# A third z buffer, unforced output transposes and norm squares on ScalarE in a planned attention and convolution kernel

## The chip, the cores and the metric

The kernel runs on the 8 cores of one Trainium2 chip. Each core takes half of the query rows of one of the four batch elements: 2048 own rows out of 4096. The cores don't exchange data. The metric is device time in microseconds (us) of the slowest core, as the median of several runs. A core has TensorE (PE, with its weight loads listed apart as PEld), VectorE (DVE), ScalarE (ACT), GpSimd (POOL) and SyncE (SP); TensorE, VectorE and ScalarE share eight banks of PSUM, each 512 float32 wide.

## What is computed

```python
h = rms_norm(x, g_pre)
q, k, v, z_a, cb, cc, cx, z_c, ga, gc = split(h @ w_in)
# branch A: 4 heads, two softmax maps each, ALiBi, causal
a = softmax(q0 @ k0.T) - lam * softmax(q1 @ k1.T)
o = rms_norm(a @ v, subln_gain) * (1 - lam_init)
y_attn = (o * silu(z_a)) @ w_attn_o
# branch B: width-3 causal depthwise convolution
u = conv3(cc * cx)
y_conv = (cb * u * silu(z_c)) @ w_conv_o
# merge
y = sigmoid(ga + b_a) * y_attn + sigmoid(gc + b_c) * y_conv
out = x + rms_norm(y @ w_out, g_post)
```

x has 4 x 4096 rows of 1024; q, k, v and z_a are 512 wide, the convolution has 512 channels.

## The kernel before

The program has four stages: normalisation and the k, q, v projections (to about 157 us in the profiled run), attention with everything of the convolution branch as filler (to about 547 us), the merge (to about 713 us), and the output projection.

The attention stage is written by a planner that runs while the program is built. It keeps an estimated clock for each engine (`p.now`), gives each instruction an estimated duration (`t=`), and so fixes the order of each engine's queue. What was estimated plays no part on the chip: there each queue runs in order and waits on semaphores.

**Groups and units.** `GROUPS` (L1038) are 16 pairs of four query blocks s and head h, in the order (3,2) (0,2) (3,3) (0,3) (3,0) (0,0) (3,1) (0,1) (2,2) and so on, numbered 0 to 15 here. A group is a run of units, each a few key blocks. The loop at L1344 emits for unit n: the scores of unit n+1 (`put_qk`, L1099), the value products of unit n (`emit_av`, L1159), filler until unit n+1's exponentials should be done (`put_fill`), then the exponentials of unit n+1 on ScalarE (L1128), with a mask on VectorE (L1140) where the unit is on the diagonal. Scores use banks 0 to 3, sums of value products banks 4 to 6. A group of s = 0 has three units, all of them masked; every other group ends in a unit without a mask.

**Filler.** `Filler` (L243) is a list of tiles; one is open at a time, and in this stage all share bank 7. A tile is some matmuls and a `post` that evicts the bank: convolution projections (L823, 8 matmuls of 512 columns, evicted at L980, L984, L1006 or, over a tanh at L1014, L1016), small halo tiles (L954), z gates (L858, 32 matmuls of 128 columns, evicted by a tanh on ScalarE, L870, and a multiply on VectorE, L872, then L878), norm tiles (L907, 16 matmuls of 2 columns), and output transposes (L1239, 4 of them, evicted at L1246). Evictions that need ScalarE are put into `hot` and emitted by `run_hot`, when the next tile opens or after the next exponentials. Taps and gates of the convolution wait in `chain`, the steps of a finished group's normalisation in `side`; `put_pieces` (L1317) places both into VectorE's free time.

**End of a group.** At a group's last unit the loop calls `drain(g - 2)`, which emits all that is left in `side` of the group two back: four sums of squares (L1213), the root (L1219, L1221, and L1223 on GpSimd), four gates (L1231), and the push of the transposes. `epilogue` (L1176) then first steps the filler until the transposes of group g - 2 are out, and emits the VectorE instructions that read banks 4 to 6 (L1186 to L1204) and so free them for the next group. z and the gates have two buffers each, by g % 2. The z tile of a group is pushed at its first unit if nothing of group g - 2 is left in `side`, else as soon as that is so.

**Norm squares and the fork.** Before group 4 (`FORK`, L1277) the program forks: if a bound on the products of the norms of k and q (heads 0 and 1) holds, a version that skips far key blocks runs. For the bound, 24 pieces of 512 columns are squared on GpSimd (L898, called from L1369 at each unit before the fork, as far as GpSimd's estimated clock allows); each four make a norm tile (L907) that is reduced on VectorE (L914); after six of these, a two-matmul tile (L931), three VectorE instructions (L938 to L943), and one register load per engine (`load_way`, L1169). At the unit before the fork a loop (L1361) makes what is still missing:

```python
if n + 1 == FORK:
    while not way:
        squares_of(1.0e9)
        fill.step()
        run_hot()
    load_way()
    p.mark()
```

The squares have two buffers, `sq[i % 2]`, and a new norm tile is inserted behind the first entry of the filler's list.

Of the kernel before, what the change touches and what calls it, by code (L numbers as in the profile page):

```python
# [289 lines left out]
def build_program():  # L290
# [23 lines left out]
    with contextlib.ExitStack() as st:  # L314
# [4 lines left out]
        def emission(p, skip):  # L319
# [90 lines left out]
            sz = [reg(sz_off + i * 2 * K, 2 * K, F32).rearrange("p (b n) -> p b n", b=4) for i in range(2)]  # L410
# [12 lines left out]
            tz_off = take(2 * K)  # L423
            tz = reg(tz_off, 2 * K, F32)
# [53 lines left out]
            for i in range(2):  # L478
                for d in range(4):
                    p.place(("hTp", i, d), htp_off[i], 8 * K)  # L480
                p.apart([("hTp", i, d) for d in range(4)])
                p.place(("prod", i), pr_off[i], 2080)
                p.place(("ut", i), u_off[i], 2 * K)
                p.place(("tt", i), t_off[i], 2 * K)
                p.place(("zr", i), zr_off[i], 2 * K)
                p.place(("sz", i), sz_off + i * 2 * K, 2 * K)
# [4 lines left out]
            p.place(("tz",), tz_off, 2 * K)  # L491
            for i in range(NR):
                p.place(("ring", i), ring_off[i], 2 * K)
# [356 lines left out]
            def z_tile(s, h, g):  # L850
                tb = g % 2
# [39 lines left out]
            def squares_of(until):  # L891

                while pieces and not kq_left and pieces[0][0] < 2 + len(normed) and p.now["pool"] < until:
                    i, t = pieces.pop(0)
                    what, h, kd = NORMS[i]
                    src = KT[h][:, kd * 2048 + t * 512:kd * 2048 + (t + 1) * 512] if what == "k" else QT[h][:, t * 512:(t + 1) * 512]
                    name = ("KT", h, kd, t) if what == "k" else ("QT", h, t)
                    p.op("pool", (lambda e, i=i, t=t, src=src: e.tensor_tensor(out=sq[i % 2][:, t * 512:(t + 1) * 512], in0=src, in1=src, op=ALU.mult)),  # L898
                         reads=[name], writes=[("sq", i % 2, t)], t=1.35)
                    if t == 3:  # L900
                        fill.q.insert(min(1, len(fill.q)), norm_tile(i))

            def norm_tile(i):
# [9 lines left out]
                def post(bk):  # L913
                    p.op("dve", (lambda e: e.tensor_reduce(out=S_NM[:, i:i + 1], in_=bank(bk)[:, 0:32], axis=mybir.AxisListType.X, op=ALU.max)),  # L914
                         reads=[("bank", bk)], writes=[("nm", i)], t=0.2)
                    normed.append(i)
                    if i == len(NORMS) - 1:
                        for a, lo, hi in ((0, 0, 4), (1, 4, 6)):
                            p.op("dve", (lambda e, a=a, lo=lo, hi=hi: e.tensor_reduce(out=S_KQ[:, a:a + 1], in_=S_NM[:, lo:hi],
                                                                                     axis=mybir.AxisListType.X, op=ALU.max)),  # L920
                                 reads=[("nm", x) for x in range(lo, hi)], writes=[("kqm", a)], t=0.15)
                        p.op("dve", (lambda e: e.tensor_scalar(out=nmb, in0=S_KQ, scalar1=1.01, scalar2=None, op0=ALU.mult)),
                             reads=[("kqm", 0), ("kqm", 1)], writes=[("nmb",)], t=0.15)
                        fill.q.insert(min(1, len(fill.q)), way_tile())
                return {"mm": mm, "post": post, "n": 16, "w": 0.057}

            def way_tile():
# [17 lines left out]
                return {"mm": mm, "post": post, "n": 2, "w": 0.057}  # L945
# [230 lines left out]
            def epilogue(s, h, g):  # L1176
                ob = g % 2
                while g >= 2 and g - 2 not in t_done:
                    fill.step()
# [46 lines left out]
                def gate(qb):  # L1226
                    while g not in z_done:
# [4 lines left out]
                                                                  in1=sz[ob][:, qb, :], op0=ALU.mult, op1=ALU.mult)),  # L1232
                         reads=[("oraw", ob, qb), ("rs", ob), ("sz", ob)], writes=[("gat", ob, qb)], t=0.345)

                def trans():
# [12 lines left out]
                    tile_ = {"mm": mm, "post": post, "n": 4, "w": 0.057}  # L1248
# [7 lines left out]
                for qb in range(4):  # L1256
                    side.append((g, 0.35, lambda qb=qb: gate(qb), [("rs", ob), ("sz", ob), ("z", g)]))
# [6 lines left out]
            def open_z(names):  # L1264

                return all(n[1] in z_done and not hot and not any(n in c_[0] for c_ in chain) for n in names if n[0] == "z")
# [28 lines left out]

            def put_fill(until):
# [6 lines left out]
                while now["pe"] < until or credit - took[0] > 0.0:  # L1303
                    if not fill.open:

                        free = p.unread(("bank", 7))
                        if hot or (free > now["pe"] + 0.15 and free + 0.2 > until):
                            break
                    if fill.left() <= TAIL:
                        break  # L1310
                    one()
# [29 lines left out]
            z_wait = None  # L1341
            put_qk(0)
            put_exp(0)
            for n in range(NU):  # L1344
                s, h, segs, first, last = units[n]
                if first:
                    started = set()
                    if g:
                        z_wait = (s, h, g)
# [3 lines left out]
                if z_wait and not any(x[0] <= g - 2 for x in side):  # L1353
                    fill.push(z_tile(*z_wait))
                    z_wait = None
# [12 lines left out]
                elif n < FORK:  # L1368
                    squares_of(now["pe"] + 0.6)  # L1369
# [245 lines left out]
```

How the kernel before makes its waits and increments, by code:

```python
    def replay(self, eng_name, engine, part, waited):  # L181
        cut = self.parting[eng_name]
        for o in self.ops[eng_name][:cut] if part == 0 else self.ops[eng_name][cut:]:
            need = {}
            for d in o.waits:
                s, v = d.token
                if v > need.get(s, 0):
                    need[s] = v
            for s in sorted(need):
                v = need[s]
                if waited.get(s, 0) >= v:
                    continue
                engine.wait_ge(self.sems[s], v)
                waited[s] = v
            ins = o.fn(engine)
            if o.token is not None:
                ins.then_inc(self.sems[o.token[0]], 16 if o.dma is not None else 1)
# [9 lines left out]
    def play(name, e):  # L207
        waited = {}
        r = e.alloc_register("way_" + name)
        fast.regs[name] = r
        fast.replay(name, e, 0, waited)
        with e.If_cmp(r, 1, "IS_GE"):
            fast.replay(name, e, 1, dict(waited))
        with e.If_lt(r, 1):
            general.replay(name, e, 1, dict(waited))
        if name == "sp":
            assert [o.token for o in fast.final_ops] == [o.token for o in general.final_ops]
            for o in fast.final_ops:
                e.wait_ge(fast.sems[o.token[0]], o.token[1])
```

## Time and profile before

| what | us |
|---|---|
| median of 3 runs (777.16 to 779.83) | 779.58 |
| the profiled execution | 780.28 |
| its span, core 4, the slowest | 778.7 |
| spans of the other cores | 772.3 to 778.1 |
| TensorE busy, core 4 | 724.1 |
| attention stage, about 157 to 547 us | 390 |

The profiled execution has 1.6 us outside the span of its slowest core. In the answers of the trace a line such as L1239 is a line of the kernel; "idle before <-" gives the time that the engine stood still before the instruction and the instruction whose end released it. PEclk is the granted clock of TensorE as a share of its full 2.4 GHz; its other level is 1.2 GHz, so 0.92 over a stretch means that part of it ran at the lower level.

### The profile page before, as it was taken

How to read it: one execution, taken by the hardware profiler on the slowest of the kernel's cores; microseconds unless marked ns; L12 is line 12 of the kernel's file. 1: busy time of each engine (PE TensorE's matmuls, PEld its weight loads, DVE VectorE, ACT ScalarE, POOL GpSimd, SP SyncE). 2: the span in 40 equal slices, each digit the busy share in tenths (PEclk: the TensorE clock that was granted, in tenths of full speed). 3: DMA queues.
4: the chain of work that ended last, by engine and by line, in shares of the span. 5: the costliest groups of instructions: out<-in, count | busy, mean ns of one | idle time of the engine just before them, and what ended most of it. 6: DMA issues, size and time to landing. Idle time of an engine off the chain costs nothing.

```text
span 778.7 us, 15293 instructions; the slowest of 8 cores (772.3 to 778.7 us)
## 1 busy us (share of the span) xinstructions
PE 724.1 (93%) x5370; PEld 382.2 (49%) x5370; DVE 368.8 (47%) x829; ACT 377.5 (48%) x552; POOL 152.5 (20%) x165
## 2 busy tenths in 40 slices
PE   4799999998888998799999999899999999999995
PEld 1354444455555454455555556555444444444442
DVE  3666444222654456657565467746522222222444
ACT  2446555264565654376666667675222222223433
POOL 1100000105711000010100001101333332321663
PEclk9999999998999999899999999999999999999998
DMA  7997973810000110000100101002852222200786
GB/s 166 246 209 203 252 168 68 128 22 2 2 2 29 28 18 12 2 15 15 29 2 2 28 2 28 3 1 56 134 123 41 41 42 40 42 1 1 247 293 221
DMA packets 39684, 57.68 MB, mean 74 GB/s; under 512 B 23825, under 2 KB 24209, under 8 KB 39346
## 3 DMA queue, kind: packets, MB, share of 16 engines
q1 hardware_dynamic: 31682, 39.58, 18.4%
q0 software_dynamic: 7776, 16.78, 13.8%
q8 instruction: 47, 0.77, 0.4%
q14 instruction: 35, 0.29, 0.1%
q10 hardware_dynamic: 144, 0.26, 0.1%
HBM read 59.76 MB, written 8.39 MB: 88 GB/s over the span
## 4 chain that ended last, share of the span: by engine, by line
PE 84%; DVE 7%; issue 4%; ACT 2%; DMA 1%; DVEq 0%; POOL 0%; SPq 0%; ACTq 0%; POOLq 0%
PE psum L1428 14%; PE psum L823 13%; PE psum L1159 12%; PE psum L725 11%; PE psum L711 8%; PE psum L1481 7%; PE psum L1435 7%; PE psum L1099 6%; PE psum L858 4%; ACT arena L1128 2%; DVE arena L1199 1%; PE psum L688 1%; DVE arena L1204 1%; PE psum L1239 1%; DMA arena<-gpre 1%
## 5 line engine op out<-in xcount | busy, mean ns | idle before, releaser
L1128 ACT ACTIVATE arena<-psum 128x1024 bf16<-128x1024 f32 (+2 forms) x259 | 219.0, 902 | 112.5 <-PE psum L1099 111.9
L1159 PE MATMUL psum<-arena 128*128 128x130 bf16 x1780 | 134.0, 223 | 5.3 <-DVE arena L1199 2.8
L1159 PEld LDWEIGHTS psum<-arena 128*128 128x128 bf16 x1780 | 106.0, 99 | 54.2 <-issue 47.9
L823 PE MATMUL psum<-arena 128*128 128x512 bf16 x512 | 126.3, 389 | 5.7 <-DVE arena L1186 2.1
L1428 PE MATMUL psum<-arena 128*128 128x512 bf16 x512 | 115.7, 379 | 0.0
L1440 ACT ACTIVATE arena<-psum,arena 128x512 f32<-128x512 f32 x64 | 44.0, 687 | 120.4 <-PE psum L1428 120.4
L1444 DVE SCALAR_TENSOR_TENSOR arena<-arena,psum 128x512 f32<-128x512 f32 x64 | 43.8, 687 | 115.8 <-PE psum L1435 115.8
L725 PE MATMUL psum<-arena 128*128 128x512 bf16 x384 | 88.4, 379 | 0.0
L1099 PE MATMUL psum<-arena 64*128 64x512 bf16 (+3 forms) x568 | 73.8, 340 | 6.3 <-ACT arena L1128 3.9
L1428 PEld LDWEIGHTS psum<-arena 128*128 128x128 bf16 x512 | 50.1, 98 | 60.2
L823 PEld LDWEIGHTS psum<-arena 128*128 128x128 bf16 x512 | 47.6, 99 | 54.9 <-issue 12.6
L711 PE MATMUL psum<-arena 128*128 128x512 bf16 x256 | 64.0, 394 | 5.2 <-DVE arena L643 4.2
L1447 POOL TENSOR_TENSOR arena<-arena 128x512 bf16<-128x512 f32 x32 | 40.4, 1262 | 116.6 <-DVE arena L1444 116.6
L1435 PE MATMUL psum<-arena 128*128 128x512 bf16 x256 | 60.5, 379 | 0.0
L725 PEld LDWEIGHTS psum<-arena 128*128 128x128 bf16 x384 | 37.0, 98 | 42.9 <-issue 0.4
L1481 PE MATMUL psum<-arena 128*128 128x512 bf16 x256 | 57.0, 387 | 0.0
L740 ACT CAST arena<-psum 128x512 bf16<-128x512 f32 x42 | 24.5, 584 | 58.5 <-PE psum L725 58.5
L1223 POOL TENSOR_TENSOR arena<-arena 128x4 f32<-128x4 f32 x16 | 18.8, 1176 | 148.1 <-DVE arena L1221 142.8
L716 DVE TENSOR_TENSOR arena<-psum,arena 128x512 bf16<-128x512 f32 x32 | 22.1, 691 | 51.6 <-PE psum L711 51.4
L645 DVE SCALAR_TENSOR_TENSOR arena<-arena 128x1024 bf16<-128x1024 f32 (+1 forms) x33 | 42.4, 1284 | 3.4
L711 PEld LDWEIGHTS psum<-arena 128*128 128x128 bf16 x256 | 25.0, 100 | 37.0 <-issue 9.8
L630 ACT ACTIVATE arena<-arena 128x1024 bf16<-128x1024 f32 (+1 forms) x33 | 34.9, 1058 | 15.1 <-DMA arena<-x_perm 15.1
(101 smaller groups left out, 626.3 us busy)
## 6 DMA issues: line engine op xcount, KB each, us to landing
arena<-x_perm SPq DMA_DIRECT2D x48, 512.0 KB, 6.4
arena<-w_chunk POOLq DMA_DIRECT2D x40, 256.0 KB, 4.8
out_own<-arena SPq DMA_DIRECT2D x15, 512.0 KB, 4.7
arena<-w_y POOLq DMA_DIRECT2D x8, 256.0 KB, 5.5
arena<-wo_r POOLq DMA_DIRECT2D x1, 2048.0 KB, 20.6
arena<-w_wide POOLq DMA_DIRECT2D x4, 256.0 KB, 11.4
arena<-w_wide POOLq DMA_DIRECT2D x1, 1024.0 KB, 11.9
arena<-gpost SPq DMA_DIRECT2D x1, 512.0 KB, 3.6
```

Of the source, the lines that this page charges most:

```text
L645: p.op("dve", (lambda e: e.scalar_tensor_tensor(out=xn[nb][0:rows, :], in0=xring[b][0:rows, :], scalar=rs0[0:rows, n:n + 1], in1=gpre[0:ro ...
L711: p.op("pe", (lambda e, kc=kc: e.matmul(bank(bk), lhsT=h_blk(n, kc), rhs=wv[kc // 2][:, kc % 2, :], start=(kc == 0), stop=(kc == KC - 1))) ...
L725: p.op("pe", (lambda e: e.matmul(bank(bk), lhsT=w[:, kc, :], rhs=rhs, start=(kc == 0), stop=(kc == KC - 1))), reads=[("w" + what, h)] + h_ ...
L823: p.op("pe", (lambda e: e.matmul(bank(bk), lhsT=lhs(kc), rhs=rhs(kc), start=(kc == 0), stop=(kc == n - 1))), reads=rd, writes=[("bank", bk)])
L1099: p.op("pe", (lambda e, kd=kd, m=m, kcol=kcol, q0=q0, c0=c0, w=w: e.matmul(psum[:, 2 * kd + m, c0 * 128:(c0 + w) * 128], lhsT=KT[h][64 * m ...
L1128: p.op("act", (lambda e, a0=a0, a1=a1, c0=c0, c1=c1, bias=bias: e.activation(out=PT[sl][:, a0:a1, c0 * 128:c1 * 128], in_=psum[:, a0:a1, c ...
L1159: p.op("pe", (lambda e, kd=kd, m=m, cb=cb, acc=acc, first=first, vj=vj: e.matmul(acc, lhsT=PT[sl][:, 2 * kd + m, cb * 128:(cb + 1) * 128], ...
L1428: p.op("pe", (lambda e, sl=sl, bk=bk, kc=kc: e.matmul(bank(bk), lhsT=ring[sl][:, kc, :], rhs=hTo[:, kc, t * 512:(t + 1) * 512], start=(kc ...
L1435: p.op("pe", (lambda e, br=br, bk=bk, c=c, src=src: e.matmul(bank(bk), lhsT=ring[sy][:, 4 * br + c, :], rhs=src[:, c, t * 512:(t + 1) * 51 ...
L1440: p.op("act", (lambda e, br=br: e.activation(out=tmp[ts[br]], in_=bank(bs[br]), func=AF.Tanh, scale=0.5, bias=bm[:, 8 * br + j:8 * br + j ...
L1444: p.op("dve", (lambda e, br=br: e.scalar_tensor_tensor(out=tmp[ts[br]], in0=tmp[ts[br]], scalar=1.0, in1=bank(bs[2 + br]), op0=ALU.add, op ...
L1481: p.op("pe", (lambda e, j=j, half=half: e.matmul(bank(b0 + half), lhsT=yT[:, j, i * 128:(i + 1) * 128], rhs=wo[:, j, half * 512:(half + 1) ...
```

## The change

It has five parts. A third z buffer of 2 KB is placed at the end of the side region; z tiles and gates take it by g % 3, and the z tile of a group is pushed at the group's first unit, always. `epilogue` no longer steps the filler until the transposes of g - 2 are out; instead a gate of group g does that before it is emitted, and `open_z` keeps gates out of VectorE's free time until then. Norm, way and transpose tiles name what they need; when a slot opens and the first tile of the list has inputs that the planner expects more than 0.1 us later, the first tile that names no needs goes ahead (`next_ready`). The squares are made on ScalarE, and the call at each unit before the fork is gone, so that the loop at the fork makes all of them; the end of the norms is told by their number. `put_fill` no longer opens a tile while bank 7 is read for more than 0.15 us to come; before it did where the bank would be free 0.2 us before the time up to which it fills.

```diff
@@ z buffers
+            NZ = 3
+            sz_at = [sz_off, sz_off + 2 * K, take(2 * K)]
+            sz = [reg(a, 2 * K, F32).rearrange("p (b n) -> p b n", b=4) for a in sz_at]
...
             def z_tile(s, h, g):
-                tb = g % 2
+                tb = g % NZ
...
             def squares_of(until):
-                while pieces and not kq_left and pieces[0][0] < 2 + len(normed) and p.now["pool"] < until:
+                while pieces and not kq_left and (pieces[0][0] < 2 or pieces[0][0] - 2 in normed) and p.now["act"] < until:
...
-                    p.op("pool", (lambda e, i=i, t=t, src=src: e.tensor_tensor(out=sq[i % 2][:, t * 512:(t + 1) * 512], in0=src, in1=src, op=ALU.mult)),
-                         reads=[name], writes=[("sq", i % 2, t)], t=1.35)
+                    p.op("act", (lambda e, i=i, t=t, src=src: e.activation(out=sq[i % 2][:, t * 512:(t + 1) * 512], in_=src, func=AF.Square)),
+                         reads=[name], writes=[("sq", i % 2, t)], t=0.58)
...
-                    if i == len(NORMS) - 1:
+                    if len(normed) == len(NORMS):
...
-                return {"mm": mm, "post": post, "n": 16, "w": 0.057}
+                return {"mm": mm, "post": post, "n": 16, "w": 0.057, "need": [("sq", i % 2, t) for t in range(4)]}
...
             def epilogue(s, h, g):
                 ob = g % 2
-                while g >= 2 and g - 2 not in t_done:
-                    fill.step()
...
                 def gate(qb):
-                    while g not in z_done:
+                    while g not in z_done or (g >= 2 and g - 2 not in t_done):
                         fill.step()
...
-                    tile_ = {"mm": mm, "post": post, "n": 4, "w": 0.057}
+                    tile_ = {"mm": mm, "post": post, "n": 4, "w": 0.057, "need": [("gat", ob, qb) for qb in range(4)]}
...
             def open_z(names):
-                return all(n[1] in z_done and not hot and not any(n in c_[0] for c_ in chain) for n in names if n[0] == "z")
+                return all(n[1] in z_done and (n[1] < 2 or n[1] - 2 in t_done) and not hot and not any(n in c_[0] for c_ in chain)
+                           for n in names if n[0] == "z")
...
+            def next_ready():
+
+                if p.when(fill.q[0].get("need", [])) > now["pe"] + 0.1:
+                    later = [k for k, t in enumerate(fill.q) if "need" not in t]
+                    if later:
+                        fill.q.insert(0, fill.q.pop(later[0]))
...
-                    if not fill.open:
-
-                        free = p.unread(("bank", 7))
-                        if hot or (free > now["pe"] + 0.15 and free + 0.2 > until):
-                            break
+                    if not fill.open and (hot or p.unread(("bank", 7)) > now["pe"] + 0.15):
+                        break
                     if fill.left() <= TAIL:
                         break
+                    if not fill.open:
+                        next_ready()
...
                     if g:
-                        z_wait = (s, h, g)
+                        fill.push(z_tile(s, h, g))
...
-                if z_wait and not any(x[0] <= g - 2 for x in side):
-                    fill.push(z_tile(*z_wait))
-                    z_wait = None
...
                 elif n < FORK:
-                    squares_of(now["pe"] + 0.6)
                     if way:
                         load_way()
```

## Rows read from the trace of the kernel before

**Rows 1.** The page: busy time by engine; shares of the chain that ended last.

```profile
PE 724.1 (93%) x5370; PEld 382.2 (49%) x5370; DVE 368.8 (47%) x829; ACT 377.5 (48%) x552; POOL 152.5 (20%) x165
...
PE 84%; DVE 7%; issue 4%; ACT 2%; DMA 1%; DVEq 0%; POOL 0%; SPq 0%; ACTq 0%; POOLq 0%
```

**Rows 2.** Busy time by stretch, core 4: stretch, length, engines, PEclk, DMA share, GB/s.

```profile
176.00:278.00 102.00, 90.98 (x966) 58.09 (x966) 48.45 (x117) 58.08 (x67) 31.14 (x32) 0.92 0.05 12
278.00:330.00 52.00, 43.00 (x371) 23.41 (x368) 33.31 (x90) 23.76 (x37) 4.00 (x7) 0.90 0.07 11
330.00:540.00 210.00, 198.08 (x2116) 120.93 (x2115) 124.74 (x357) 142.36 (x175) 19.75 (x28) 1.00 0.08 13
36.00:176.00 140.00, 140.00 (x762) 65.85 (x761) 63.90 (x103) 71.18 (x133) 5.65 (x12) 1.00 0.72 151
```

**Rows 3.** PE's waits, 174 to 278: line, releaser, us in total, times, longest.

```profile
PE psum L907 <- DVE arena L962: 2.3, 1, 2.3
PE psum L1099 <- DVE arena L943: 1.8, 1, 1.8
```

**Rows 4.** In order of time, GpSimd's squares, then three VectorE instructions: start, us.

```profile
175.66 8.65 POOL L898 TENSOR_TENSOR arena<-arena 128x512 bf16<-128x512 bf16 x8 [23.92 <-PE psum L725]
...
180.62 1.35 DVE L1140 TENSOR_TENSOR arena<-arena 128x512 bf16<-128x512 bf16 x1 [0.22 <-ACT arena L1128]
181.89 1.52 DVE L878 TENSOR_TENSOR arena<-arena 128x512 f32<-128x512 f32 x1
...
226.83 0.68 DVE L878 TENSOR_TENSOR arena<-arena 128x512 f32<-128x512 f32 x1
```

**Rows 5.** In order of time, PE at the first norm tile: start, us, [idle before].

```profile
184.06 0.62 PE L907 MATMUL psum<-arena 128*128 128x2 bf16 x16 [2.29 <-DVE arena L962]
...
187.74 3.36 PE L823 MATMUL psum<-arena 128*128 128x512 bf16 x8
```

**Rows 6.** In order of time, ScalarE and PE around the fork.

```profile
276.93 1.08 ACT L1128 ACTIVATE arena<-psum 128x512 bf16<-128x512 f32 x2
277.83 0.71 PE L1099 MATMUL psum<-arena 64*128 64x384 bf16 x8
278.63 1.28 ACT L1128 ACT_TABLE_LOAD   x1 [0.62 <-PE psum L1099]
...
281.55 1.89 PE L823 MATMUL psum<-arena 128*128 128x512 bf16 x8 [0.72 <-DVE arena L1186]
```

**Rows 7.** In order of time, ScalarE: four 512-column exponentials; the first output block.

```profile
290.66 2.06 ACT L1128 ACTIVATE arena<-psum 128x512 bf16<-128x512 f32 x4 [0.40 <-PE psum L1099]
...
716.72 1.02 ACT L1490 ACTIVATE arena<-psum 128x1024 bf16<-128x1024 f32 x1 [4.49 <-PE psum L1481]
...
717.97 1.28 ACT L1506 ACT_TABLE_LOAD   x1
```

**Rows 8.** PE at the bound's last step; SyncE's register load and its next instruction.

```profile
232.18 0.27 PE L931 MATMUL psum<-arena 128*1 128x128 bf16 x2
...
235.16 1.04 PE L1099 MATMUL psum<-arena 64*128 64x512 bf16 x4 [1.84 <-DVE arena L943]
...
L1169 SPq TENSOR_LOAD <-arena x1: 467/467/467, 234.4 to 234.4; - x1
...
235.03 0.33 SPq L530 DMA_DIRECT2D arena<-gpost  x1
```

**Rows 9.** In order of time, the ends of groups 4 and 5: PE, then VectorE.

```profile
301.87 0.38 PE L1239 MATMUL psum<-arena 128*128 128x128 bf16 x4 [2.47 <-DVE arena L872]
...
319.48 3.57 PE L823 MATMUL psum<-arena 128*128 128x512 bf16 x8 [0.68 <-DVE arena L1186]
...
299.71 1.14 DVE L1231 SCALAR_TENSOR_TENSOR arena<-arena 128x128 bf16<-128x128 f32 x4 [1.35 <-POOL arena L1223]
...
319.25 0.16 DVE L1186 TENSOR_REDUCE arena<-psum 128x6 f32<-128x12 f32 x1
```

**Rows 10.** PE's waits, 278 to 547: line, releaser, us in total, times, longest.

```profile
PE psum L1239 <- DVE arena L872: 7.0, 4, 3.6
```

More of the change, by code:

```diff
@@ L409, in emission @@
             sz_off = take(4 * K)
-            sz = [reg(sz_off + i * 2 * K, 2 * K, F32).rearrange("p (b n) -> p b n", b=4) for i in range(2)]
             gc_off = take(16 * K)
@@ L485, in emission @@
                 p.place(("zr", i), zr_off[i], 2 * K)
-                p.place(("sz", i), sz_off + i * 2 * K, 2 * K)
             p.place(("wz",), wz_off, 8 * K)
@@ L491, in emission @@
             p.place(("tz",), tz_off, 2 * K)
+            for i in range(NZ):
+                p.place(("sz", i), sz_at[i], 2 * K)
             for i in range(NR):
@@ L944, in post @@
                                     reads=[("prodn",)], writes=[("way",)], t=0.15))
-                return {"mm": mm, "post": post, "n": 2, "w": 0.057}
+                return {"mm": mm, "post": post, "n": 2, "w": 0.057, "need": [("nmb",)]}
             def halo_tile(c):
@@ L1231, in gate @@
                     p.op("dve", (lambda e: e.scalar_tensor_tensor(out=gat[ob][:, qb, :], in0=oraw[ob][:, qb, :], scalar=RS[:, qb:qb + 1],
-                                                                  in1=sz[ob][:, qb, :], op0=ALU.mult, op1=ALU.mult)),
-                         reads=[("oraw", ob, qb), ("rs", ob), ("sz", ob)], writes=[("gat", ob, qb)], t=0.345)
+                                                                  in1=sz[g % NZ][:, qb, :], op0=ALU.mult, op1=ALU.mult)),
+                         reads=[("oraw", ob, qb), ("rs", ob), ("sz", g % NZ)], writes=[("gat", ob, qb)], t=0.345)
                 def trans():
@@ L1256, in epilogue @@
                 for qb in range(4):
-                    side.append((g, 0.35, lambda qb=qb: gate(qb), [("rs", ob), ("sz", ob), ("z", g)]))
+                    side.append((g, 0.35, lambda qb=qb: gate(qb), [("rs", ob), ("sz", g % NZ), ("z", g)]))
                 side.append((g, 0.0, trans, []))
@@ L1352, in emission @@
                     drain(g - 2)
-                if z_wait and not any(x[0] <= g - 2 for x in side):
-                    fill.push(z_tile(*z_wait))
-                    z_wait = None
                 credit += max(0.0, fill.left() + late - TAIL - credit) * work[n] / rest_work
```

## The prediction

> **What bounds the kernel now.** First the page: TensorE is busy for 724.1 of 778.7 us and carries 84% of the chain that ended last [rows 1]. So only TensorE's idle time and its time at the lower clock can be won or lost. Then the table by stretch, for where these lie: from 36 to 176 us TensorE never stops (140.00 of 140.00), and the change touches nothing there; the loss is in attention [rows 2]. I split that stage in three, each loss being idle time plus what the granted clock took, worked out as length times (1 - PEclk):
> - 176 to 278, up to the fork: 11.0 idle and 8.2 of clock, 19.2 us.
> - 278 to 330, groups 4 and 5: 9.0 idle and 5.2 of clock, 14.2 us.
> - 330 to 540: 11.9 idle, no clock, which is 5.7% and serves as the norm for undisturbed attention.
>
> Last TensorE's waits, for what ended the idle time. Before the fork they are those around norm tiles and the register load [rows 3], afterwards above all the transposes that wait for VectorE [rows 10].
>
> **The squares before the fork: removed.** Eight squares hold GpSimd for 8.65 us, and there are three such runs [rows 4]. Meanwhile VectorE's two-input instructions take about twice as long: L878 takes 1.52 us beside them and 0.68 without [rows 4]. One such delay holds the bank under the first norm tile, which stands 2.29 us [rows 5]; behind it eight matmuls of 512 columns take 3.36 us [rows 5] against 1.89 [rows 6], which is the 1.2 GHz level. All this goes, and so does the 1.84 us wait for the register load in this place [rows 8]. What can be won at most is the stretch's loss less the norm: 19.2 - 0.057 x 79 (102 less the loss and some 4 us of norm tiles) = 14.7 us. From below: the two waits of rows 3 with what the clock took from the tile behind the first (3.36 - 1.89 = 1.5) make 4.1 + 1.5 = 5.6, say 6. The ends of groups 0 to 2 remain in either kernel, so I take 10.5.
>
> **The squares at the fork: added.** The call at each unit is gone, so all 24 pieces are emitted by the loop ahead of the fork, that is behind the exponential at 276.93 and ahead of the scores at 277.83 [rows 6]. Neither the next scores nor the value products of the last unit of group 3 are emitted until the loop ends: this is a serial chain between ScalarE, TensorE and VectorE, with nothing of attention beside it.
> - Squares: four 512-column exponentials take 2.06 us [rows 7], 0.52 each, so eight take 4.2 us. The row reads PSUM and the squares read SBUF; the first output block's Square takes 1.02 for 1024 columns [rows 7], so twice the number is excluded. Two buffers allow eight pieces at once, hence three rounds, 12.6 us.
> - The list then holds one convolution tile, norm tile 1, norm tile 0, the next convolution tile, and so on: four convolution tiles, T0 to T3, six norm tiles (0.62 each [rows 5]) and the way tile.
> - Between rounds: last square, the rest of a norm tile, its reduction, the first matmuls of the other norm tile, ScalarE again. A reduction of 0.2 us and four semaphore crossings of about 0.1 come to 1.2 us. Meanwhile the convolution tile and its eviction must also be done: at the lower clock 3.36 + 0.95 for the copy and its semaphores, with a norm reduction ahead, which is 0.4 longer than the squares. So 1.6, twice.
> - End: two norm tiles with reductions, 1.9; T3 at 3.36 with 0.95; the way tile's 0.27, and from its end at 232.45 to TensorE's next start behind the load 2.71 in the row [rows 8], of which some 0.85 is queueing and other work on VectorE. I take 1.9.
>
> Sum: 12.6 + 3.2 + 1.9 + 4.3 + 0.3 + 1.9 = 24.2, and 25 with one tanh eviction that has to queue behind squares on ScalarE. TensorE does useful work in it: 4 x 1.73 of convolution (a row of 1.89 less the drain) and 3.6 of norm and way tiles, which the old kernel does too: 10.5. The loss is 14.5 us, and about 2.5 for the restart at the lower clock, since the tile behind the wait in rows 9 loses 3.57 - 1.89 = 1.7 by itself. I take 17. Bounds: 11, if the clock stays up (T3 1.5 less, the gaps 0.8 less), no tanh stands in it (0.8 less) and the restart costs nothing: 25 - 3.1 - 10.5; 22, if every round ends in a tanh behind squares and the restart takes 4.
> The branch right after the load costs little: SyncE's load begins at 234.4 and takes 0.467, and its next instruction, which stands behind the fork, starts at 235.03 [rows 8].
>
> Does Square need another function table? The first output block's Square at 716.72 follows the merge's tanh without a table load, and the load of 1.28 comes only ahead of the square root [rows 7]. So none is added. The Trainium skill, ScalarE: Activation LUTs, section Table sets: the hidden batching unit, asks to group calls by table set, because each switch costs about 2.7 us, and its table does not name the set of Square. By that rule, with Square in a set of its own, two switches would add some 5.3 us to the chain and give 789 us; the row speaks against it.
>
> **Unforced transposes, z first, the third buffer.** The buffer itself costs 2 KB and no instruction. z first is the same work earlier. The transposes waited 7.0 us for z's eviction, 2.47 and 3.6 of it at the ends of groups 4 and 5 [rows 9, 10]; behind each a fill tile waits 0.68 and then runs at the lower clock [rows 9]. Gross, that is most of the 14.2 us of this stretch. What is late next is VectorE: at the last unit `drain(g - 2)` still emits sums of squares, root and gates ahead of the epilogue, and the gates wait 1.35 for GpSimd's root [rows 9]. The next group's value products wait for that epilogue, at 319.25 in group 5 [rows 9]; without the z multiply and the transposes' copy ahead of it, it comes about 1.9 earlier, no more. TensorE then stands there instead of ahead of the transposes. I take +1 for group 4, +2 for group 5 and +3 for the smaller waits later. Floor 0; ceiling 12, which is 14.2 less the norm for 38 us.
>
> The new wait, a gate of g for the transposes of g - 2, finds them done: they have a whole group more, and behind a gate on VectorE's queue stand only the epilogue and the mask of the next unit.
>
> **No opening on a busy bank.** Where the planner waited for bank 7 under an epilogue, it filled that time: at 281.55 it stood 0.72 and then worked 1.89 [rows 6]. Now it breaks, and TensorE stands until scores or sums are free, some 1.8. I charge 1.1 each for groups 1, 3 and 7 and 0.2 for smaller places: 3.5. Bounds 0 and 5. With the 6 above, the two parts together give +2.5, bounds -5 and +12. `next_ready` costs nothing: norm tiles are only stepped by the fork's loop, which does not call it, and a transpose that is passed over loses nothing.
>
> **The sum.** Against the profiled 780.28: -10.5 (squares gone) + 17 (chain at the fork) - 2.5 (ends of groups) = +4.0, 784.3. The median of the runs is 0.7 lower, so on its terms 783.6 us.
>
> **Rivals.**
> - *The ends of groups pay in full, and it is faster.* z no longer sits in bank 7 when the transposes want it, VectorE finds time for a finished group's steps before the last unit, and the clock doesn't fall. For it: VectorE is busy for only 33.31 of 52 us there [rows 2]. Against it: the root's trip to GpSimd stands in VectorE's queue. It pays 12 instead of 2.5: -10.5 + 17 - 12 = -5.5, 774 us. It decides from a gain above 10.4 at these ends, where the sum passes -3.9.
> - *The chain is covered, and nothing much changes.* The clock stays up and the fork costs its lower bound: -10.5 + 11 - 2.5 = -2, 778 us. For it: three of the four tiles run while ScalarE squares. Against it: TensorE works for 10.5 us of 22 at best, and PEclk fell before the fork already where it stood for 2.29 us [rows 5].
> - *The stall moves to the epilogue everywhere.* Groups end on VectorE, fill is refused there, and before the fork only the lower bound comes back: 17 - 6 + 3 = +14, 794 us.
>
> **How the numbers follow.** Forecast 0.50, with a range of its own of 778 to 789; ends pay in full 0.24; covered chain 0.13; stall at the epilogue 0.13. A measurement of this kernel tells about 0.5%, 3.9 us, from no change, so faster means below 775.7 and slower above 783.5. Of the forecast 0.27 lies above, 0.22 within and 0.01 below; the rival at 774 gives 0.19 to faster and 0.05 to no change, that at 778 0.03 and 0.10, that at 794 all to slower. Faster 0.23, same 0.37, slower 0.40. The range reaches to the rivals on both sides, 773 to 793, and leaves out the far halves of both.
>
> **What would show it.** Between two exponentials at about 275 (the fork comes some 10 us earlier) ScalarE has 24 squares in three runs of eight, with 20 us or more from the first to the register load, and TensorE is idle for 12 or more of the 25. Before it, L878 and L1140 keep their short times, PEclk is near 1.00, and no norm tiles lie between units. At the ends of groups 4 and 5 the waits of transposes are gone and value products wait for L1199 and L1204. I would be wrong if convolution tiles filled the fork, if the clock stayed up through it, or if the ends of groups had no wait at all.

## The result and the profile after

The changed kernel takes 813.4 us (median of 4 runs, 811.25 to 814.58) against 779.4 before: 1.0439 times as long, 95% interval 1.0408 to 1.0470, 34 us slower. Here and below a time is the median of a kernel's fast executions; in a few others the cores of one die ran at a lower granted clock and took over 30 us longer, and some expectations quote a median that takes one of these in and lies up to 1 us higher. The forecast was 783.6 and its range ended at 793. The sign was right, the size wrong by a factor of eight.

The page of after has the lines that answer to [rows 1]:

```profile
PE 729.0 (90%) x5370; PEld 388.8 (48%) x5370; DVE 363.7 (45%) x829; ACT 388.7 (48%) x576; POOL 126.2 (16%) x141
...
PE 79%; ACT 6%; issue 5%; DVE 5%; DMA 3%; POOL 0%; DVEq 0%; SPq 0%; ACTq 0%; POOLq 0%
```

TensorE works as long as before (729.0 against 724.1), but 82 us of the span are idle, where 55 were, and ScalarE now has 6% of the chain. Lines are 3 higher than before in this kernel, by some lines less: L826 is the old L823, L1102 the old L1099, L1131 the old L1128, L1162 the old L1159, L1200 the old L1199, L1240 the old L1239.

The table by stretch of after, as in [rows 2]: stretch, length, engines, PEclk, DMA share, GB/s. The cuts are the start of the loop at the fork, its end, the end of groups 4 and 5, and the last value product.

```profile
157.00:263.00 106.00, 98.85 (x1011) 58.68 (x1010) 46.41 (x113) 68.46 (x77) 4.95 (x8) 1.00 0.04 7
263.00:293.00 30.00, 19.80 (x168) 9.13 (x166) 6.76 (x22) 15.05 (x29) 1.24 (x3) 0.61 0.14 22
293.00:350.00 57.00, 42.76 (x405) 29.37 (x403) 29.20 (x86) 27.47 (x42) 3.49 (x5) 0.81 0.02 8
350.00:563.00 213.00, 186.46 (x1989) 117.55 (x1988) 116.70 (x340) 136.15 (x169) 17.35 (x25) 0.98 0.07 11
563.00:581.00 18.00, 18.00 (x87) 8.20 (x85) 13.90 (x37) 1.70 (x3) 3.21 (x7) 1.00 0.30 56
```

The fourth line is the surprise: 213 us of plain attention with 26.5 us idle, where the old kernel lost 11.9 of 210 [rows 2]. TensorE's waits say to what. Before first, then after (line, releaser, us in total, times, longest):

```profile
PE psum L1099 <- ACT arena L1128: 3.9, 12, 1.0
PE psum L1159 <- DVE arena L1199: 2.8, 5, 1.1
```

```profile
PE psum L1102 <- ACT arena L1131: 27.8, 45, 1.8
PE psum L1162 <- DVE arena L1200: 14.1, 7, 4.1
```

Scores now wait 45 times for the exponentials that free their banks, and value products seven times for the epilogue. Transposes no longer appear, where they waited 7.0 us for z [rows 10]. One of the 45, in order of time on PE (start, us, [idle before]):

```profile
310.09 1.89 PE L826 MATMUL psum<-arena 128*128 128x512 bf16 x8
311.81 0.39 PE L1162 MATMUL psum<-arena 128*128 128x130 bf16 x4
312.14 0.61 PE L1102 MATMUL psum<-arena 64*128 64x512 bf16 x4
312.67 0.63 PE L1162 MATMUL psum<-arena 128*128 128x130 bf16 x8
315.05 0.61 PE L1102 MATMUL psum<-arena 64*128 64x384 bf16 x8 [1.75 <-ACT arena L1131]
```

VectorE evicts the convolution tile of 310.09 from 312.91 to 313.60, so its bank is still read when the next slot comes at 313.3. No tile is opened, so TensorE has nothing to do until 315.05. What was not done is left for the end of attention. Again before, then after:

```profile
540.12 7.07 PE L823 MATMUL psum<-arena 128*128 128x512 bf16 x32
```

```profile
562.97 17.43 PE L826 MATMUL psum<-arena 128*128 128x512 bf16 x80
```

Four tiles were left before, ten are now. From the fork's table load on ScalarE, the last value product, and the first merge matmul, the 33.2 us by which the merge starts later split as follows (tiles are convolution tiles of 8 matmuls):

| kernel | to the fork's load | tiles by then | from there to the last value product | tiles in it | tiles at the end | merge starts |
|---|---|---|---|---|---|---|
| before | 278.6 | 14 | 261.4 | 46 | 4 | 547.0 |
| after | 292.8 | 19 | 270.1 | 35 | 10 | 580.2 |

So 14.2 us are lost up to the fork, for which five tiles (8.6 us) more are done; behind the fork attention takes 8.7 us longer and does eleven tiles (19 us) less; six more stand at the end and take 10.4 us.

### The profile page after: what moved, and what is told of

The parts are those of the page before. It is cut to its first block, busy times and chain, and to the rows that moved or that the text cites. A ratio compares the mean times of both kernels' runs of the same rounds, so it can differ in the third digit from the quotient of the medians.

```text
span 811.1 us, 15249 instructions; the slowest of 8 cores (805.0 to 811.1 us)
## 1 busy us (share of the span) xinstructions
PE 729.0 (90%) x5370; PEld 388.8 (48%) x5370; DVE 363.7 (45%) x829; ACT 388.7 (48%) x576; POOL 126.2 (16%) x141
## 4 chain that ended last, share of the span: by engine, by line
PE 79%; ACT 6%; issue 5%; DVE 5%; DMA 3%; POOL 0%; DVEq 0%; SPq 0%; ACTq 0%; POOLq 0%
PE psum L1431 14%; PE psum L826 13%; PE psum L1162 10%; PE psum L728 10%; PE psum L1484 7%; PE psum L1438 7%; PE psum L1102 6%; PE psum L714 6%; ACT arena L1131 5%; PE psum L861 4%; DMA arena<-w_wide 2%; DMA arena<-x_perm 1%; ACT arena L901 1%; DVE arena L1200 1%; PE psum L691 0%
## 5 line engine op out<-in xcount | busy, mean ns | idle before, releaser
L1131 ACT ACTIVATE arena<-psum 128x1024 bf16<-128x1024 f32 (+2 forms) x259 | 217.2, 904 | 84.9 <-PE psum L1102 84.2
L1162 PE MATMUL psum<-arena 128*128 128x130 bf16 x1780 | 134.8, 224 | 19.8 <-DVE arena L1200 14.1
L1162 PEld LDWEIGHTS psum<-arena 128*128 128x128 bf16 x1780 | 105.8, 99 | 65.7 <-issue 61.8
L826 PE MATMUL psum<-arena 128*128 128x512 bf16 x512 | 126.2, 394 | 1.7 <-DVE arena L917 1.3
L1102 PE MATMUL psum<-arena 64*128 64x512 bf16 (+3 forms) x568 | 75.5, 337 | 30.0 <-ACT arena L1131 27.8
L826 PEld LDWEIGHTS psum<-arena 128*128 128x128 bf16 x512 | 48.9, 100 | 53.5 <-issue 8.7
L1102 PEld LDWEIGHTS psum<-arena 64*128 64x128 bf16 x568 | 21.2, 94 | 66.9 <-issue 60.2
```

The source lines that it names most:

```text
L826: p.op("pe", (lambda e: e.matmul(bank(bk), lhsT=lhs(kc), rhs=rhs(kc), start=(kc == 0), stop=(kc == n - 1))), reads=rd, writes=[("bank", bk)])
L1102: p.op("pe", (lambda e, kd=kd, m=m, kcol=kcol, q0=q0, c0=c0, w=w: e.matmul(psum[:, 2 * kd + m, c0 * 128:(c0 + w) * 128], lhsT=KT[h][64 * m ...
L1131: p.op("act", (lambda e, a0=a0, a1=a1, c0=c0, c1=c1, bias=bias: e.activation(out=PT[sl][:, a0:a1, c0 * 128:c1 * 128], in_=psum[:, a0:a1, c ...
L1162: p.op("pe", (lambda e, kd=kd, m=m, cb=cb, acc=acc, first=first, vj=vj: e.matmul(acc, lhsT=PT[sl][:, 2 * kd + m, cb * 128:(cb + 1) * 128], ...
```

## Experiments

Ratios are to the kernel before on the same chip. The seven kernels of the table give, with before, all combinations of three parts: z with the transposes (z, three buffers, unforced transposes and `next_ready`, which no run takes apart), the opening rule, and the squares at the fork. A difference between two runs is good to about 3 us.

| parts | run | us | ratio, 95% interval |
|---|---|---|---|
| z | e4 | 779.9 | 1.0004 (0.9991 to 1.0017) |
| rule | e2 | 793.9 | 1.0182 (1.0151 to 1.0212) |
| fork | e3 | 796.2 | 1.0212 (1.0188 to 1.0236) |
| z, rule | e5 | 788.7 | 1.0122 (1.0097 to 1.0147) |
| z, fork | e1 | 786.6 | 1.0080 (1.0053 to 1.0106) |
| rule, fork | e6 | 815.7 | 1.0482 (1.0449 to 1.0514) |
| all | after | 813.4 | 1.0439 (1.0408 to 1.0470) |

**The old opening rule in the changed kernel (e1).**

```diff
-                    if not fill.open and (hot or p.unread(("bank", 7)) > now["pe"] + 0.15):
-                        break
+                    if not fill.open:
+                        free = p.unread(("bank", 7))
+                        if hot or (free > now["pe"] + 0.15 and free + 0.2 > until):
+                            break
```

> The changed kernel with one part undone: put_fill opens a tile on a busy bank 7 again where the planner holds it free 0.2 us before the time up to which it fills. Theory A, the new opening rule is the cause: while the program is built, the old rule opened 38 of 105 tiles on a bank that the planner held busy, and on the chip TensorE stood only 5.7 us ahead of such tiles; the new rule refuses all of them, TensorE then waits for exponentials (L1131, 27.8 us against 3.9) and ten tiles instead of four are left for the end. Then this run gives back most of the 34 us: 784 to 792 us, waits for L1131 back under 8 us, four tiles at the end. Theory B, the rule costs only the 3.5 us that I charged, and VectorE's work at the ends of groups and the fork cost the rest: 808 to 812 us.

786.6 us: 27 of the 34 us are back. PE's waits (columns as above):

```profile
PE psum L1102 <- ACT arena L1131: 7.8, 15, 1.1
PE psum L1162 <- DVE arena L1200: 7.7, 3, 4.4
```

The waits for exponentials fall from 27.8 to 7.8, those for the epilogue by half, and three tiles stand at the end. Theory A holds, B falls.

**The new opening rule alone (e2).** The mirror of that edit on the kernel before.

> The kernel before with one part of the change alone: no opening on a busy bank 7. Theory A: 794 to 804 us, with the waits for exponentials well above 15 us and eight or more convolution tiles left for the end of attention. Theory B: 780 to 784 us.

793.9 us, at the lower edge of theory A (794). PE's waits, and the end of attention in order of time:

```profile
PE psum L1099 <- ACT arena L1128: 23.9, 41, 1.8
```

```profile
537.45 1.30 PE L1159 MATMUL psum<-arena 128*128 128x130 bf16 x20
538.58 22.61 PE L823 MATMUL psum<-arena 128*128 128x512 bf16 x102
```

The last value products come no later than before (538.98 there), but twelve to thirteen tiles stand behind them instead of four. The rule by itself doesn't slow attention down: it leaves its slots empty, and the tiles are paid in full afterwards.

**The squares at the fork alone (e3).**

```diff
                 elif n < FORK:
-                    squares_of(now["pe"] + 0.6)
```

with the squares on ScalarE as in the change.

> The kernel before with one part of the change alone: norm squares on ScalarE, all of them made by the loop at the fork. By the two terms of the prediction, which hold if the trace of after is read rightly there (24.7 us from the first convolution tile to the register load): 17 us for the chain less 10.5 us won before the fork, 786 us, 783 to 790. Rival, nothing is won before the fork because the old norm tiles only filled time in which TensorE waits anyway: 793 to 797 us. Second rival, the chain is cheap since its tiles are missing later: 778 to 782.

796.2 us: the first rival's number, for another reason than the rival's. The loop starts 10.0 us earlier than in the old kernel (267.8 against 277.8), and 19 convolution tiles are done by then, against 14 there, so more was won before the fork than I expected. The loop's chain takes 26.5 us. But the 60 us behind it lose more than in the old kernel. Up to the loop, the loop, and behind it (stretch, length, engines, PEclk, DMA share, GB/s):

```profile
176.00:267.70 91.70, 87.92 (x908) 52.22 (x904) 47.06 (x113) 58.70 (x69) 6.53 (x11) 1.00 0.08 13
267.70:294.30 26.60, 16.47 (x130) 7.24 (x130) 6.04 (x18) 13.26 (x26) 0.19 (x1) 0.66 0.00 1
294.30:354.30 60.00, 45.31 (x367) 25.73 (x368) 32.59 (x94) 22.72 (x36) 3.89 (x6) 0.78 0.09 19
```

Behind it 14.7 us are idle and 13.2 go to the clock, where the 60 us from 278 in the old kernel lost 9.1 and 5.4. At the end of group 5, on PE:

```profile
338.57 3.57 PE L858 MATMUL psum<-arena 128*128 128x128 bf16 x32 [4.04 <-DVE arena L1016]
343.92 0.59 PE L1239 MATMUL psum<-arena 128*128 128x128 bf16 x4 [1.78 <-DVE arena L872]
```

**The same with VectorE's steps emitted ahead of the loop (e11).**

```diff
                 if n + 1 == FORK:
+                    drain(g - 1)
                     while not way:
```

> The kernel before with the squares on ScalarE at the fork (796.5 us), and with drain(g - 1) ahead of the loop, so that sums of squares, root and gates of group 2 are emitted onto VectorE's queue while the loop runs. In the 60 us behind the fork the run without it lost 28 us to idle time and clock, before 14.5, with waits of 4.0 and 1.8 at z and transposes at the ends of groups 4 and 5. Theory: the loop leaves VectorE's steps undone, and they collide with the forced transposes afterwards; then 788 to 792 us, and those waits at the end of group 4 gone. Rival, tiles used up early are what is missing: 794 to 798 us.

785.7 us, 1.0077 (1.0053 to 1.0100): 10.5 us back, 2 us more than the range allowed. The chain itself gets longer, as PE first waits for the gates that now lie ahead:

```profile
275.22 1.05 PE L1239 MATMUL psum<-arena 128*128 128x128 bf16 x4 [5.30 <-DVE arena L1231]
```

and the fork's table load comes at 300.3 instead of 295.5. But from there to the last value product it takes 248.4 us instead of 263.0. So the fork costs 16.5 us alone because its loop emits none of a finished group's steps while VectorE is nearly idle (6.04 busy of 26.60 us in e3's loop), and these then collide with the forced z and transposes of groups 4 and 5. With them out of the way the fork costs 6 us.

**z and transposes alone (e4).** The changed kernel with the old rule and the squares back on GpSimd at each unit.

> The changed kernel with the old opening rule and the squares back on GpSimd at each unit, so three z buffers, z at a group's first unit, unforced transposes and next_ready alone. By the prediction's term 6 us less than before at the ends of groups 4 and 5 and after: 773 to 776 us. Rival, VectorE's queue at the end of a group takes the whole gain: 778 to 781, with the waits for L1199 and L1204 as long as those of the transposes were. Theory B for the 34 us would put this run above 790.

779.9 us, no change: the rival. PE's waits:

```profile
PE psum L1162 <- DVE arena L1200: 6.6, 6, 3.2
PE psum L826 <- DVE arena L1247: 3.4, 5, 0.7
```

The transposes' waits for z fall from 7.2 us in the whole run before to 1.0, and value products wait for the epilogue instead, up to 3.2 us, where the old kernel's longest was 1.1. The stall moved along VectorE's queue. Beside the fork the same part is worth 9.6 us (e3 to e1), where there is the collision of e11 to take away.

**z with the rule (e5), and the rule with the fork (e6).** e5 is the changed kernel with the squares back on GpSimd at each unit; e6 is the kernel before with the edits of e2 and e3.

> The changed kernel with the squares back on GpSimd at each unit: z, transposes and the new opening rule, without the chain at the fork. Theory A2, the parts add up (14.2 for the rule alone, 0.4 for z and transposes alone): 792 to 797 us. Rival, the rule costs 26 us wherever the transposes are unforced, as between the changed kernel and the run with the old opening rule: 803 to 808 us.

> The kernel before with the new opening rule and the squares at the fork, without z and transposes. Theory A2, the parts add up (14.2 and 16.8): 808 to 813 us, that is nearly all of the changed kernel's loss. Rival, the two losses are in part the same tiles (the rule leaves tiles for the end, the fork uses tiles up early), so that together they cost less: 797 to 804 us.

e5 took 788.7 us, 5 less than the parts add up to; e6 took 815.7, some 6 more than they do. Neither the sums nor the rivals came: the rule's price depends on what it stands beside. With z alone it is 9 us, by itself 14, with the fork 19, with both 27.

**VectorE's steps ahead of the loop in the changed kernel (e13).** The edit of e11 on the changed kernel.

> The changed kernel with drain(g - 1) ahead of the loop at the fork. On the kernel before with the squares at the fork this gave 10.7 us back. If the same collision stands in the changed kernel: 801 to 805 us. Rival, z early and unforced transposes had removed it already (with the fork they gave 8.9 us, 796.5 to 787.6): 810 to 814 us.

811.6 us, 1.0422 (1.0402 to 1.0441): the rival. The fork's load comes 3.0 us later than in the changed kernel (295.8), and from there to the last value product it takes 4.4 us less (265.8), not 14.6 as in e11. So most of that collision is gone in the changed kernel, and draining ahead of the loop only pays for itself.

**Where the rule takes its 26 us (e14, e15).** `put_fill` gets a flag for the call behind the epilogue; e14 uses the new rule in all other calls, e15 in that one alone.

```diff
-            def put_fill(until):
+            def put_fill(until, end=False):
...
+                        if hot or (free > now["pe"] + 0.15 and (not end or free + 0.2 > until)):
```

> The changed kernel with the new opening rule inside groups and the old one in the call behind the epilogue. The changed kernel takes 813.4 us, with the old rule everywhere 787.6. My prediction put the rule's price at the ends of groups. If it is there: 788 to 796 us, with the waits for L1200 (14.1 us in the changed kernel) halved. If it is inside groups: 804 to 812 us, with the waits for exponentials (L1131) still above 20 us.

> The mirror of the run before: the new rule only in the call behind the epilogue, the old one inside groups. If the price is inside groups: 787 to 795 us, with waits for exponentials below 12 us. If it is at the ends: 804 to 812 us. If the two runs together give back clearly more or less than the 26 us, the two places share it, and neither alone is the cause.

e14 took 799.6 us (1.0273, 1.0252 to 1.0294), between its two ranges; e15 793.1 (1.0166, 1.0145 to 1.0188), in the range for a price inside groups. Against 786.6 the rule costs 13 us inside groups, 6.5 at their ends, and 7 more where both stand. e14's and e15's waits:

```profile
PE psum L1102 <- ACT arena L1131: 24.4, 37, 1.8
```

```profile
PE psum L1162 <- DVE arena L1200: 12.0, 7, 4.4
PE psum L1102 <- ACT arena L1131: 9.1, 19, 1.6
```

Each place has its own wait. That the two add up to 19.5 and not 27 is not explained by these runs.

**A milder rule (e12), and an earlier estimate (e10).**

```diff
-                    if not fill.open and (hot or p.unread(("bank", 7)) > now["pe"] + 0.15):
+                    if not fill.open and (hot or p.unread(("bank", 7)) > now["pe"] + 0.5):
```

> The kernel before with the new opening rule alone, but with 0.5 us in place of 0.15: 24 of the 38 tiles that the old rule opened on a bank held busy, those with the shortest expected wait, open again. The run with 0.15 took 793.9 us. If each refusal costs the same, two thirds of the 14 us come back: 783 to 786 us. Rival, the few tiles with long waits are those that cost, since their slots are the long ones: 789 to 793 us. Second rival, refusing only long waits is the better rule: below 779 us.

787.0 us, 1.0095 (1.0074 to 1.0116): between the first two ranges. Two thirds of the tiles opened again give back half of the 14 us.

```diff
-                        free = p.unread(("bank", 7))
+                        free = p.unread(("bank", 7)) - 0.35
```

> The kernel before with the planner's estimate of bank 7 set 0.35 us earlier in the old opening rule, so that more tiles open. On the chip the 38 tiles that were opened on a bank held busy stood 0.15 us each, where the planner expected 0.51. Theory P, the estimate is too late and slots are lost by it: 772 to 777 us. Rival, opening more tiles late pushes scores and exponentials back: 781 us or more.

783.0 us, 1.0038 (1.0023 to 1.0053): the rival. So opening earlier by 0.35 us loses 3 us, and the two rules tried that refuse more (e2, e12) lose as well. But 0.35 came from a wrong reading. The 5.7 us that the expectations name stand ahead of the 18 convolution tiles among the 38, 0.32 each; ahead of all 38 TensorE stood 12.4 us, 0.33 each where the planner expected 0.51. Its estimate is late by 0.18, and no run tried that.

**No convolution filler in attention (e9).** All halo and convolution tiles are put into the list only behind the last unit.

> The kernel before with all convolution and halo tiles taken out of the attention stage and put at its end, where they run back to back on eight banks; only z, transposes, norm and way tiles are left as filler. It measures what filler costs in its slots. If every tile costs its 1.73 us wherever it stands, as my prediction held (TensorE bounds the stage): attention gets 104 us shorter and the end 104 longer, 780 to 790 us. If a tile in a slot is free, because the unit would wait for its exponentials anyway: attention keeps its length, 60 x 1.73 more at the end, 875 to 885 us. The run before with 8 tiles fewer behind the fork took as long there (262 against 261 us), which is nearer to the second: I expect 830 to 870 us.

814.1 us in one run, 16 us below what I expected. The table by stretch:

```profile
157.00:470.00 313.00, 258.10 (x3097) 176.25 (x3096) 134.00 (x445) 227.91 (x278) 41.96 (x39) 0.95 0.03 6
470.00:581.00 111.00, 111.00 (x558) 50.97 (x557) 85.76 (x151) 8.96 (x15) 16.62 (x32) 1.00 0.25 34
```

Sixty tiles moved out of the slots cost 34.7 us in all, 0.58 each. Of a tile's 1.73 us a slot hides 0.58 on average, about a third. Neither of the two theories holds: two thirds of a tile's time are paid in its slot, and one third falls into time in which TensorE would stand anyway. In this run's first stretch it stands 28.0 us for exponentials and 10.2 for the epilogue.

**The squares on ScalarE, but at each unit (e8).**

```diff
-                    p.op("pool", (lambda e, i=i, t=t, src=src: e.tensor_tensor(out=sq[i % 2][:, t * 512:(t + 1) * 512], in0=src, in1=src, op=ALU.mult)),
-                         reads=[name], writes=[("sq", i % 2, t)], t=1.35)
+                    p.op("act", (lambda e, i=i, t=t, src=src: e.activation(out=sq[i % 2][:, t * 512:(t + 1) * 512], in_=src, func=AF.Square)),
+                         reads=[name], writes=[("sq", i % 2, t)], t=0.58)
```

> The kernel before with the squares on ScalarE, but called at each unit as before, as far as ScalarE's estimated clock allows. It tells the engine from the place. If the place (the chain at the fork) is what costs 16.8 us: 776 to 782 us, with VectorE's L878 back at 0.68 us and no wait of 2.29 at the first norm tile. If ScalarE is the wrong engine, because the squares push exponentials late: 788 us or more, with the waits for L1128 up by 8 us.

773.3 us, 0.9934 (0.9911 to 0.9957): below the range, and faster than both kernels. On PE at the place of [rows 5]:

```profile
180.44 0.55 PE L954 MATMUL psum<-arena 128*128 128x32 bf16 x16
181.74 0.81 PE L823 MATMUL psum<-arena 128*128 128x512 bf16 x3 [0.74 <-DVE arena L962]
```

The wait of 2.29 us is 0.74, no tile near it takes 3.36, and the fork's table load comes at 273.1 instead of 278.6. So the loss of e3 came from the place, not from the engine.

**z and the squares at each unit (e7).** The changed kernel with the edits of e1 and of e8.

> The changed kernel with the old opening rule and with the squares on ScalarE called at each unit: the two parts of the change that cost nothing in the runs so far, together. If they add up (squares per unit 0.993 of before, z and transposes 1.000): 772 to 776 us. Rival, z early helps only where the fork has left VectorE's steps undone, and otherwise its added waits for L1200 show once the squares' delays are gone: 777 to 781 us.

775.4 us, 0.9945 (0.9927 to 0.9963): in the first range, but no better than e8. Of the change, moving the squares to ScalarE is worth keeping, at each unit; z and transposes add nothing to it.

## Why the prediction was wrong

**The opening rule: the step that failed.** The prediction charged 1.1 us each at three group ends and 0.2 for smaller places, 3.5 in all, with an upper bound of 5. It is 14 alone and 27 in the change. Without it the change costs 6 to 7 us (e1), where the other terms came to 0.5. Two things were wrong with it.
- *The count.* I took the places from TensorE's waits for bank 7 in the trace, a few of them long enough to see, like the 0.72 us in [rows 6]. But the rule acts on the planner's clock. When the program is built, the old rule opens 38 of 105 tiles on a bank that the planner holds busy for more than 0.15 us. In the trace of before TensorE stands ahead of 17 of them for more than 0.2 us, and ahead of the other 21 for less, so they could not be picked out by their waits. The new rule refuses all such; in the changed kernel it does so 51 times where the old rule would have opened a tile. The planner in the kernel's source could have counted them.
- *The price.* I set the wait for the bank against the tile. But in a slot TensorE has nothing else to do: scores wait for their banks, value products for exponentials. Refusing a tile doesn't save the wait for the bank, it turns the slot into a wait for ScalarE (45 such waits, where there were 12), and the tile is paid later in full. e12 shows it where the waits are real: the 14 tiles that it refuses had 9.9 us of waits ahead of them in the kernel before, and refusing them costs 7.4 us.

**The squares before the fork: the mechanism held, the term was too small.** 10.5 us were expected, at most 14.7. In e3 idle time and clock from 176 us to the loop fall from 19.1 to 3.8 us, 15.3 less: the loop starts 10.0 us earlier and five tiles (8.6 us) more are done by then, while the norm and way tiles (some 4 us) are still to come. GpSimd's part is confirmed by e8. (The 24 squares of [rows 4] ran in groups of ten, six and eight, not three of eight.)

**The chain at the fork: the chain held, what it leaves behind was missing.** Expected were three rounds, 25 us. In after, ScalarE (start, us) and then PE:

```profile
263.92 1.08 ACT L1131 ACTIVATE arena<-psum 128x512 bf16<-128x512 f32 x2
264.88 4.27 ACT L901 ACTIVATE arena<-arena 128x512 bf16<-128x512 bf16 x8
270.31 4.26 ACT L901 ACTIVATE arena<-arena 128x512 bf16<-128x512 bf16 x8 [1.17 <-PE psum L910]
276.91 4.26 ACT L901 ACTIVATE arena<-arena 128x512 bf16<-128x512 bf16 x8 [2.33 <-PE psum L910]
...
292.79 1.28 ACT L1131 ACT_TABLE_LOAD   x1 [10.95 <-PE psum L1102]
```

```profile
265.04 1.89 PE L826 MATMUL psum<-arena 128*128 128x512 bf16 x8 [0.37 <-DVE arena L875]
270.98 3.57 PE L826 MATMUL psum<-arena 128*128 128x512 bf16 x8 [0.44 <-DVE arena L917]
277.57 3.57 PE L826 MATMUL psum<-arena 128*128 128x512 bf16 x8 [0.44 <-DVE arena L917]
284.93 3.57 PE L826 MATMUL psum<-arena 128*128 128x512 bf16 x8 [0.44 <-DVE arena L917]
...
291.67 1.03 PE L1102 MATMUL psum<-arena 64*128 64x384 bf16 x8 [1.85 <-DVE arena L946]
```

Eight squares take 4.27 us (4.2 expected), four tiles of which three run at the lower clock (3.57; PEclk 0.61 in the stretch), and 26.6 us lie between the first tile and the next scores. TensorE is idle for 9.9 us of them, where the prediction named 12 or more; the rest of the loss is the clock. No table load stands ahead of the squares; the one at 292.79 is the fork's own, as before. So the row on Square was read rightly. The rule of the Trainium skill about switches, in ScalarE: Activation LUTs, section Table sets: the hidden batching unit, does not bear on this change: both kernels have four table loads in all.

With what is won ahead of it, the fork should have cost 6.5 us (17 - 10.5). It costs that where nothing is left undone on VectorE (6 in e11, 6.7 beside z, e4 to e1) and 16.5 without. In e3 the fork's load comes 16.8 us later than before, but nine tiles (15.6 us at 1.73) more are done by then. The loss lies behind it, where attention takes 1.6 us longer (263.0 to the last value product) with eight tiles (13.8 us) fewer. The prediction had 2.5 us there, for the restart. It named what the loop keeps TensorE and ScalarE from, but not that `put_pieces` isn't called in it either.

**The ends of groups: what is late next was right, the gain was not.** The forecast was a gain of 6 us before the rule's charge, with VectorE's epilogue as what is late next. In e4 the waits do move to L1200, but they take the whole gain (0.3 us slower than before); a gain shows only beside the fork, 9.6 us.

**The rivals.** The third, the stall that moves to the epilogue, comes nearest (794 us), in its time and in part in its reason: fill is refused and value products wait for L1200, but it had the refusal at the ends of groups, where e15 finds the smaller part.

## What to carry to other kernels

Where the order of work is planned, a rule that refuses filler must be priced in the planner's own terms: count how many slots it empties, and charge each what the engine then waits for and what the tile costs at the end, not the wait that it avoids. A work item that is moved to a serial point must be looked at for what else is not emitted meanwhile, on every queue. And a helper engine that slows its neighbour is worth replacing, but in the place where it was: the same squares on ScalarE gain 0.7% at each unit and lose 2% in one block.

## What the runs showed of the hardware

GpSimd's products slow VectorE more widely than the two-input instructions of [rows 4]. A VectorE instruction with one tensor input, in before beside GpSimd's squares, and then in e8, where GpSimd is idle (start, us):

```profile
197.73 1.26 DVE L994 TENSOR_SCALAR arena<-arena 128x512 f32<-128x512 f32 x1
```

```profile
191.58 0.48 DVE L994 TENSOR_SCALAR arena<-arena 128x512 f32<-128x512 f32 x1
```

Of the sixteen L994 in before, the two beside squares take 1.26 us, the others 0.475 to 0.482. The Trainium skill, SBUF — State Buffer, section Who interferes with whom, says that a VectorE instruction with two SBUF inputs contends with a GpSimd instruction that reads SBUF, and that one in a two-port mode, which a scalar multiply can enter, contends with GpSimd for a port pair that the first to issue holds to its end. The traces agree in that both kinds lose: 1.26 against 0.48 for the one, 1.52 against 0.68 for the other [rows 4], and in e8 all sixteen L878 take between 0.681 and 0.686 us. Whether L994 ran in a two-port mode no trace shows.
